# First layer of a two-layer decoder on one core: order of the input product, of the short-range keys and queries, and how x reaches the product

## What is computed

```python
def rms_norm(x, g):
    xf = xf * lax.rsqrt(jnp.mean(xf * xf, axis=-1, keepdims=True) + EPS)
    return (xf * g.astype(jnp.float32)).astype(x.dtype)

def first_block(...):                    # h is x, 256 x 2048
    a = rms_norm(h, attn_norm[l])
    proj = a @ w_in[l]                   # 2048 x 2368
    # proj is cut into c_q (512), c_kv (512), the shared key before rotation (64),
    # short-range queries (16 heads of 64), keys (2 of 64) and values (2 of 64)
    ...
def swa_sink_attention(q, k, v, positions, rel_bias, sinks):
    ...
    bucket = t5_bucket(pos[:, :, :, None] - pos_band[:, :, None, :])
    bias = rel_bias.astype(jnp.float32)[bucket]
    s = s + bias
    ...
    m = jnp.maximum(jnp.max(s, axis=-1, keepdims=True), sink)
    e = jnp.exp(s - m)
    p = e / (jnp.sum(e, axis=-1, keepdims=True) + jnp.exp(sink - m))
```

## Time and profile before

| | us |
|---|---|
| median of 3 runs | 2589.64 (2587.62 to 2589.89) |
| the profiled execution's own time | 2588.41 |
| its span | 2586.6 |
| TensorE busy (99%) | 2559.7 |
| VectorE busy (64%) | 1656.9 |
| ScalarE busy (52%) | 1348.3 |

### The profile page before, as it was taken

The page is one execution under the profiler, slowest core; times in us unless marked ns, Lnnn a source line. Parts: engine busy times, 40 slices in busy tenths (PEclk is TensorE's granted clock), DMA queues, the critical chain, the costliest instruction groups (busy, mean ns, idle before and its releaser), DMA issues.

```text
span 2586.6 us, 33899 instructions
## 1 busy us (share of the span) xinstructions
PE 2559.7 (99%) x13798; PEld 2158.8 (83%) x13798; DVE 1656.9 (64%) x2124; ACT 1348.3 (52%) x1919; POOL 0.2 (0%) x4
## 2 busy tenths in 40 slices
PE   9999999999999999999999999999999999999998
PEld 7878888888888888887888888888888888888887
DVE  6686566655665567568788967544556655665565
ACT  6565554444444446568866665544444444444444
POOL 0000000000000000000000000000000000000000
PEclk9999999999999999999999999999999999999999
DMA  6534666565556555555454437544565655556554
GB/s 224 163 131 147 208 226 203 194 195 188 191 192 195 190 186 178 195 179 179 130 190 147 147 131 252 179 146 143 192 192 191 194 194 189 189 194 195 190 187 144
DMA packets 235682, 470.79 MB, mean 182 GB/s; under 512 B 8235, under 2 KB 17670, under 8 KB 234118
## 3 DMA queue, kind: packets, MB, share of 16 engines
q1 hardware_dynamic: 234390, 467.04, 55.0%
q10 hardware_dynamic: 1136, 1.58, 0.2%
HBM read 462.30 MB, written 6.29 MB: 181 GB/s over the span
## 4 chain that ended last, share of the span: by engine, by line
PE 49%; DVE 1%; ACT 0%; issue 0%; DVEq 0%
PE ps L1235 10%; PE ps L1237 10%; PE ps L1236 10%; PE ps L1274 9%; PE ps L1273 5%; PE ps L1613 1%; PE ps L1793 1%; PE ps L1768 1%; PE ps L1292 0%; PE ps L1667 0%; PE ps L1551 0%; PE ps L1542 0%; PE ps L1704 0%; PE ps L1594 0%; PE ps L1690 0%
## 5 line engine op out<-in xcount | busy, mean ns | idle before, releaser
L2589 DVE TENSOR_TENSOR WL<-Wt,WH 128x1024 fp32r<-128x1024 f32 (+1 forms) x861 | 1037.7, 1210 | 710.3 <-ACT WH L1848 659.6
L1848 ACT ACTIVATE WH<-Wt 128x1024 fp32r<-128x1024 f32 (+1 forms) x861 | 894.5, 1046 | 768.1 <-PE ps L1237 507.4
L1235 PE MATMUL ps<-WH,XT 128*128 128x512 f32 (+1 forms) x1184 | 470.5, 397 | 0.7 <-DVE XT L2598 0.4
L1235 PE MATMUL ps<-WH,HT 128*128 128x512 f32 (+2 forms) x1176 | 457.0, 389 | 3.2 <-DVE WL L2589 3.2
L1237 PE MATMUL ps<-WH,XT 128*128 128x512 f32 (+1 forms) x1184 | 459.3, 388 | 0.0
L1236 PE MATMUL ps<-WL,XT 128*128 128x512 f32 (+1 forms) x1184 | 458.7, 387 | 0.0
L1237 PE MATMUL ps<-WH,HT 128*128 128x512 f32 (+2 forms) x1176 | 451.5, 384 | 0.0
L1236 PE MATMUL ps<-WL,HT 128*128 128x512 f32 (+2 forms) x1176 | 451.1, 384 | 0.0
L1274 PE MATMUL ps<-XT,WH 128*128 128x512 f32 x960 | 336.5, 394 | 0.0
L1274 PE MATMUL ps<-HT,WH 128*128 128x512 f32 x960 | 336.5, 394 | 0.0
L1273 PE MATMUL ps<-HT,WL 128*128 128x256 f32 x960 | 266.6, 278 | 0.0
(11 more groups left out here) (395 smaller groups left out, 1890.4 us busy)
## 6 DMA issues: line engine op xcount, KB each, us to landing
Wt<-in_mlp_w SPq DMA_DIRECT2D x128, 1024.0 KB, 5.2
Wt<-in_w_up SPq DMA_DIRECT2D x64, 1024.0 KB, 5.2
Wt<-in_w_down SPq DMA_DIRECT2D x64, 1024.0 KB, 5.0
Wt<-in_w_in SPq DMA_DIRECT2D x53, 1024.0 KB, 5.1
Wt<-in_w_out SPq DMA_DIRECT2D x32, 1024.0 KB, 5.1
Wt<-in_xa_wk SPq DMA_DIRECT2D x16, 1024.0 KB, 5.1
Wt<-in_xa_wv SPq DMA_DIRECT2D x16, 1024.0 KB, 5.1
Wt<-in_xa_wq SPq DMA_DIRECT2D x16, 1024.0 KB, 5.1
```

What stands on the lines that cost most here:

```text
L1235: pe.matmul(o, xh, wh, start=start, stop=False)
L1848: act.activation(m.WH[:, i % NR, 0:2 * w], m.Wt[:, slot % NW, h * 2 * w:(h + 1) * 2 * w], ACT.Copy).then_inc(*up("wsplit.a", i))
L2589: dve.tensor_tensor(m.WL[:, i % NR, 0:2 * w], m.Wt[:, slot % NW, h * 2 * w:(h + 1) * 2 * w], m.WH[:, i % NR, 0:2 * w].bitcast(F32), SUB).t ...
```

## The change

It consists of these parts.

- **x turned outside.** A second copy of x, `in_xt`, is laid out with the tokens across before the launch. It is loaded into XTR. `first_rows` makes high (ScalarE) and low (VectorE) part from SBUF; no transposes of x and no PSUM banks for them. The copies in H are no longer loaded at the start.
- **Squares.** `first_squares`: ScalarE squares four tiles of XTR at once (128x1024), four times; VectorE adds them up, three additions of 128x1024; `first_sums`: eight PE matmuls of 128x1 against a column of ones; VectorE copies two columns.
- **Chunks.** The narrow chunk comes first (h0 to h7), then 1024, 1536, 0, 512.
- **Eviction.** `ev_win` no longer holds up the plan when the norm isn't there yet; it comes as a background step.
- **Keys, rotation, queries.** `gen_keys` runs beside `gen_bias`: `swa_keys` right after h10, the shared key's rotation when chunk 1024 and the angles are there, queries when chunk 1536 is. Before, all of it stood behind the bias in one generator.
- **One more half** between `swa_divide` and `swa_turn`.
- **Loads.** SyncE's first slots are 320 wide, and each 512 KB piece of XTR is issued behind the weights of its slot, where the piece of H stood ahead of them. ScalarE's queue has XTR where H was.

```diff
+        self.SQS = arena("SQS", [P, 4, 256], 18944)
+        self.SQ = [arena(f"SQ{i}", [P, 4, 256], 23040 + 4096 * i) for i in range(2)]
+        self.XTR = arena("XTR", [P, KT, 256], 35328)
...
-    p.add("w_in", A["w_in"], (0, KT), [(1024, 512), (1536, 512), (2048, 320), (0, 512), (512, 512)])
+    p.add("w_in", A["w_in"], (0, KT), [(2048, 320), (1024, 512), (1536, 512), (0, 512), (512, 512)])
...
-    p.do("warm", 2, *p.banks(1))
-    turn_in = chain(*(norm_chunk(p, "ln1", c) for c in range(4)))
+    p.do("warm", 3, *p.banks(1))
     p.do("split_first", 0)
     p.split = 1
-    next(turn_in)
-    p.do("warm", 2, *p.banks(1))
+    p.do("first_rows", 0)
     p.do("split_first", 1)
+    p.do("first_rows", 1)
     p.split_to(1)
-    next(turn_in)
-    p.bg.append(turn_in)
+    p.do("first_rows", 2)
+    for kt in range(6):
+        p.now("ln1", kt)
+
+    def gen_first():
+        for pr in range(3, 8):
+            p.do("first_rows", pr)
+            p.now("ln1", 2 * pr)
+            p.now("ln1", 2 * pr + 1)
+            if pr in (4, 6):
+                p.do("first_squares", pr // 2 - 2)
+            yield
+        for c in (2, 3):
+            p.do("first_squares", c)
+            yield
+        p.do("first_sums", *p.banks(1))
+        yield
+        p.do("norm_scale", "ln1")
+        p.now("ln1", "scale")
+        yield
+
+    p.bg.append(gen_first())
...
-    def gen_swa():
-        while not p.had("proj", 4) or not p.had("ln1", "scale"):
+    def gen_keys():
+        while not p.had("proj", 4):
+            yield
+        yield
+        p.do("swa_keys", *p.banks(1))
+        yield
+        while not p.had("proj", 2) or not p.had("angles"):
             yield
         p.do("rope_products", "k")
...
         p.do("krope_turn", *p.banks(1))
         p.now("krope")
         yield
-        p.do("swa_keys", *p.banks(1))
-        yield
+        while not p.had("proj", 3):
+            yield
         for pr in range(4):
             p.do("swa_queries", pr, *p.banks(1))
             if pr % 2:
                 yield
         p.do("swa_sinks")
+        p.now("queries")
+        yield
+
+    def gen_swa():
+        while not p.had("queries"):
+            yield
...
             p.do("swa_divide", par, hg)
             yield
             yield
+            yield
             p.do("swa_turn", par, hg, *p.banks(2))
...
     def ev_win(ci, c0, w, acc, i):
-        ci = (ci + 2) % 5
-        p.until(("ln1", "scale"))
-        p.do("ev_win", ci, c0, w, acc, i)
-        p.now("proj", ci)
-        if ci in (0, 1):
-            p.bg.insert(0, chain(one_step(), norm_chunk(p, f"ln_c{ci}", 0)))
+        ci = (4, 2, 3, 0, 1)[ci]
+
+        def late():
+            while not p.had("ln1", "scale"):
+                yield
+            p.do("ev_win", ci, c0, w, acc, i)
+            p.now("proj", ci)
+            if ci in (0, 1):
+                p.bg.insert(0, chain(one_step(), norm_chunk(p, f"ln_c{ci}", 0)))
+
+        eviction = late()
+        if next(eviction, "end") != "end":
+            p.bg.append(eviction)
...
+    @named
+    def first_rows(pr):
+        on.wait_ge(*at(*first_sig(pr)))
+        on.wait_ge(*at("prep.v", "gain0"))
+        for kt in (2 * pr, 2 * pr + 1):
+            act.activation(m.turned("ln1", 0, kt), m.XTR[:, kt, :], ACT.Copy, scale=m.g1("attn_norm", kt)).then_inc(
+                *up("ln1.a", "high", kt))
...
+            dve.tensor_tensor(m.SQS[:, :, :], m.SQS[:, :, :], m.SQ[c % 2][:, :, :], ADD).then_inc(
+                *up("ln1.v", "squares", c))
...
         for slot in range(NW):
             dst, src = weights(slot)
-            if slot:
-                a = 1024 + 512 * (slot - 1)
-                sp.dma_start(m.H[:, :, a:a + 512], x[:, :, a:a + 512]).then_inc(*dma(f"ld_x{slot + 1}"))
             for h in range(slot == 0, 2):
                 sp.dma_start(dst[:, 2 * h:2 * h + 2, :], src[:, 2 * h:2 * h + 2, :]).then_inc(*dma(f"wfirst{slot}{h}"))
+            if slot:
+                kt = 4 + 4 * slot
+                sp.dma_start(m.XTR[:, kt:kt + 4, :], A["xt"][:, kt:kt + 4, :]).then_inc(*dma(f"ld_xt{kt // 2}"))
```

More of the change, by code:

```diff
@@ L620, in gen_bias @@
         p.do("angle_parts")
+        p.now("angles")
         yield
@@ L746, in plan_all @@
     p.bg.append(chain(gen_prep(), gen_bias(), gen_swa()))
+    p.bg.append(gen_keys())
     p.product("w_in", ev_win, of_norm("ln1"))
@@ L1280, in norm_turn, with first_sums @@
     @named
+    def first_sums(b):
+        bk = m.bank(b)
+        for s in freed(b):
+            on.wait_ge(*s)
+        on.wait_ge(*at("ln1.v", "squares", 3))
+        on.wait_ge(*at("prep.v", "one"))
+        for tb in range(2):
+            for i in range(4):
+                t = pe.matmul(bk[:, tb:tb + 1], m.SQS[:, i, tb * P:(tb + 1) * P], m.small("one", 1), start=i == 0,
+                              stop=i == 3)
+        t.then_inc(*up("ln1.t", "sums"))
+    @named
     def norm_turn(nm, c, pr, b):
@@ L1283, in norm_turn @@
         for tb in range(2):
-            for s in [("ld_x0a",), ("ld_x0b",)][pr:pr + 1] if (nm, c) == ("ln1", 0) else normed_sigs(nm, c, tb):
+            for s in normed_sigs(nm, c, tb):
                 on.wait_ge(*at(*s))
@@ L1854, in norm_turn @@
         on.wait_ge(*at(nm + ".t", c, pr))
-        on.wait_ge(*at("prep.v", "gain0" if nm == "ln1" else "columns"))
+        on.wait_ge(*at("prep.v", "columns"))
         for kt in (k0, k0 + 1):
@@ L2566, in begin @@
         dve.memset(m.WARM[:, :], 0.0).then_inc(*up("prep.v", "warm"))
+        dve.memset(m.small("one", 1), 1.0).then_inc(*up("prep.v", "one"))
     @named
@@ L2600, in norm_turn, with first_rows, first_squares, first_sums @@
                 *up(nm + ".v", "done", kt, frees=b))
+    @named
+    def first_rows(pr):
+        for kt in (2 * pr, 2 * pr + 1):
+            on.wait_ge(*at("ln1.a", "high", kt))
+            dve.scalar_tensor_tensor(m.turned("ln1", 1, kt), m.XTR[:, kt, :], m.g1("attn_norm", kt),
+                                     m.turned("ln1", 0, kt).bitcast(F32), MUL, SUB).then_inc(*up("ln1.v", "done", kt))
+    @named
+    def first_squares(c):
+        if c:
+            on.wait_ge(*at("ln1.a", "square", c))
+            if c > 1:
+                on.wait_ge(*at("ln1.v", "squares", c - 1))
+            else:
+                on.wait_ge(*at("ln1.a", "square", 0))
+            dve.tensor_tensor(m.SQS[:, :, :], m.SQS[:, :, :], m.SQ[c % 2][:, :, :], ADD).then_inc(
+                *up("ln1.v", "squares", c))
+    @named
+    def first_sums(b):
+        on.wait_ge(*at("ln1.t", "sums"))
+        dve.tensor_copy(m.small("ln1.ss", 2), m.bank(b)[:, 0:2]).then_inc(*up("ln1.v", "sum", frees=b))
     @named
@@ L2627, in norm_scale @@
             on.wait_ge(*last(sig))
-        dve.tensor_reduce(ss, m.small2(nm + ".sums", n), AX, ADD).then_inc(*up(sig, "sum"))
+        if nm != "ln1":
+            dve.tensor_reduce(ss, m.small2(nm + ".sums", n), AX, ADD).then_inc(*up(sig, "sum"))
         if nm == "lnmix":
@@ L2789, in rope_products @@
         if c == "k":
-            on.wait_ge(*at("bias.v", "end"))
+            on.wait_ge(*at("bias.v", "distance"))
             dve.memset(m.KZ[:, :, 0:64], 0.0).then_inc(*up("rope.v"))
@@ L2834, in swa_spare @@
         on.wait_ge(*at("bias.a", "end"))
-        on.wait_ge(*at("ln1.a", "squares"))
     @named
```

26 lines of the change are left out of this document (18 added, 8 removed).

## The result

The changed kernel takes 2602.53 us (median of five runs, 2600.34 to 2604.50), the kernel before 2589.64. The ratio is 1.0051 with a 95% interval of 1.0040 to 1.0063: slower by 12.9 us, 0.5%. The forecast was 2594.5 with a range up to 2600, so both are too low.

What follows compares the result with a forecast made beforehand. TensorE's work bounds the kernel, with VectorE's queue limiting h0 to the keys. h11 at 39.8 + 157.2 carried over + 0.7 rotation + 8.25 second pass puts h54 at 206.0 against 199.84, so 2594.5 us, range 2582 to 2600.

Steps and rivals of the forecast that it cites:

- The likeliest case: Whole kernel: h54 at 206.0 against 199.84, so 2594.5 us; chance 0.58, of it 0.30 same and 0.28 slower.
- Start: Before h0: x needs no turning by TensorE, so h0 starts at 7.3 instead of 10.46, 3.2 us earlier.
- VectorE's chain: From gain copy to keys' copy: 30.5 us of queued VectorE work limits TensorE, so h11 starts at 39.8, bounds 37 and 42.
- 2.7 in sum: VectorE's queue before the keys' copy: its waits for slots and ScalarE's high parts and squares, 2.7 us in all.
- First sums: Eight 128x1 matmuls on TensorE: 0.85 us, bounds 0.3 to 1.3.
- The clock: Whole stretch on TensorE: taken as the full one, 1.00 in the window's row; waits priced without any loss of clock.
- The rest carried over: From h11 to h54: 189.38 before less 32.1 of work and waits already done or gone leaves 157.2 us.
- the second pass: Short-range attention, h41 to behind h51: new waits at scores, splits, turning and values add 8.25 us, bounds 4 and 10.
- 0.7 at the rotation: Beside the bias after h11: the rotation's sums come late once, 0.7 us, bounds 0 and 1.5.
- R1: VectorE reaches the keys in time and second-pass round trips are covered: faster, 2582 us (2578 to 2586); chance 0.14.
- R2: Only one of the keys' delay and the second-pass waits goes: 2586 to 2591 us, no change; chance 0.16.
- R3: Loads limit the start, making h8's split late by 1 to 4 us: 2595.5 to 2598.5, 2602 at most; chance 0.12.

Runs made afterwards that it cites:

- Two edits to the second pass's timing: Changed kernel, second head group one half later in the second pass: 2601.65 us; x-alone kernel, extra matmuls, c_kv turning later, weights first, one more half there: 2588.81 us.
- the first two edits: Against the changed kernel: convolution rows issued ahead of a 1024 KB weight slot, 2604.09 us; short-range keys two halves later, 2604.14 us.
- the kernel with the heads held: Changed kernel with heads beginning behind h32 and the extra half ahead of the turning undone; keys, rotation and queries stay early: 2598.60 us.

## Why the prediction was wrong, step by step

**The direction, and where.** The likeliest case was slower than before by 4.9 us, with "same" and "slower" nearly even, and all the loss ahead of h54. The sign and the place are right, the size is not: 12.9.

**Start, right.** h0 at 7.3 was forecast and is 7.19. Its first six matmuls stand 0.27 us apart and the next 0.15, so h0 runs partly at the lower level. It costs little here: h1 waits for its weights until 11.58. The number is partly luck: the gain was copied at 5.10 and not at 6.19, and h0 came 2.1 us behind it, not 1.1, since three matmuls on the zeroed tile stood ahead of it in TensorE's queue and took from 4.82 to 7.19.

**VectorE's chain, right in its work and wrong in its waits.** 30.5 us of work against 30.84. The term that failed is "2.7 in sum" for waits, which were 7.3, and so h11 starts at 43.94 instead of 39.8, beyond the bound of 42, although the chain began 1.1 earlier. VectorE was to be busy over 90% from 10 to 39 us and was so for 24.0 of 29.0 us, 83%. The largest part, 2.5 us, is VectorE waiting for TensorE's first sums. They were late because of the columns, a step of which I had costed only its work. The change pulls TensorE's start and the narrow halves (1.76 us each) ahead, while the convolution's rows come when SyncE has worked through the small loads and a weight slot. A wait of a moved step on its DMA was left out of the sum. Taking it away alone gave 1.9 us at h12, of which the edit accounts for perhaps 0.8, and nothing at the end: VectorE's 2.5 us went, and shorter waits came for them. So the wait for the columns is the largest single piece of the 7.3, but the keys' delay doesn't hang on it alone.

**First sums, too cheap.** 0.85 was taken of 0.3 to 1.3; they take 1.7, beyond the upper bound, in every kernel that has them. Each matmul is two instructions in the trace, and the bound had counted eight.

**The clock, missing altogether.** I read the clock of 1.00 as a property of the kernel. It held there with TensorE standing at most 1.6 us at a time. The forecast itself had it stand 2 to 4 us at the keys and in the gaps of the second pass, and priced this as the wait alone. In the profile, h7, h11 and h43 carry 4.2 us more.

**The rest carried over and the second pass, right apart from the clock.** From the start of h11 to h54 the forecast has 157.2 + 0.7 + 8.25 = 166.15. It was 169.38, 3.2 more. The clock of h11 and h43 is 2.7 of that. Of the waits read from the order, 1.85 at the bank is 1.93, 0.35 is 0.54, 0.65 is 0.78, 0.7 at the rotation is 0.92, and 2.0 at the values is 1.87.

**The rivals.** R1 (VectorE in time) and R2 did not come. R1's price was also summed wrongly: with h11 at 37 and 2 to 4 us for the second pass the forecast's own terms put h54 at 197 to 199, which is 2585 to 2588, and not at 194. So the lower end of the range had nothing behind it. R3 (loads limit the start) has the right place: VectorE is idle ahead of the low parts of h0's second weight tile and of h1's, for weights. But it looked at the fourth slot, and what held TensorE was a small load. Its upper price, 2602, near to what was measured, adds more than its terms give (1.75 us from the pass's upper bound make it 2600), so that this is no hit.

**What adds up.** h11 came 4.1 us later than forecast and the stretch from there to h54 took 3.2 more; 2594.5 + 4.1 + 3.2 is 2601.8, against 2601.9 for the profiled execution. That is where the error lies, and no check of the causes. For these the experiments stand: the order by itself costs 15 us, and x turned outside by itself costs nothing.

**Open.** Why the clock stays low for 3 us in one execution and 10 us in another in the second pass of the same instructions is not settled: extra matmuls in the longest wait did not hold it up. It also falls where TensorE stood 0.8 us or less: with the keys two halves later it is 0.72 from 156 to 162 us, behind a wait of 0.5. The changed kernel and three others whose order differs only behind h12 have h12 at 48.1 (the changed one), 49.0, 49.8 and 49.8; in the last two the clock is at 0.54 from 23 to 38 us. A single profile of this stretch is therefore good to some 2 us.

## What to carry to other kernels

A wait that is put on TensorE costs itself and may cost the half behind it 1.2 to 1.5 us: it did here behind waits of 3.7, of 2.8 and of 1.9 and 0.8 us, and didn't behind those of 1.5 to 1.6 in the kernel before. In a sum such a wait needs both terms, the second with a chance. When a step moves ahead in time, list what each of its instructions waits for, DMAs of some 50 KB in a queue behind a megabyte included, not only the work that it brings. Taking a wait out of one place often only moves it. The comparison put behind the keys lost its 3.2 us within 28 us. Two edits to the second pass's timing ended with 3.4 us behind h51, in place of the waits at the scores in one and of 2.3 us behind h49 in the other. The leads of the first two edits lasted to h42 and were lost to the clock.

## What was not expected of the hardware

- Matmuls with one moving column: eight in float32 are 16 instructions and take 1.7 us (0.11 each). In one kernel the clock was at 0.59 and 0.55 in the 4 us behind them, though TensorE had been busy but for 0.5 us; three more matmuls directly behind them kept it up in three kernels of three.
- The granted clock falls in the same gap for 3 us in one program and 10 us in the next, and the executions of the changed kernel lie further apart, 4.2 us over five, against 2.3 for the kernel before. That the first is the reason for the second is likely, and not shown: the kernel with the heads held varied by 0.4 us over four.
- Reading from SBUF in place of PSUM brought VectorE nothing in the new place either: a pair of low parts of x takes 0.87 to 0.88 us busy, as before.
